# Five start offsets for the block weights of a two-block transformer kernel

## The reference, cut to what matters

```python
h = h + 0.5 * swiglu(rms_norm(h, ffn1_norm[i]), ffn1_w_in[i], ffn1_w_out[i])

def swiglu(x, w_in, w_out):
    g, u = jnp.split(x @ w_in, 2, axis=-1)      # w_in is 1024 x 5632: the up projection
    return (jax.nn.silu(g) * u) @ w_out         # w_out is 2816 x 1024: the down projection
```

## Time and profile before

| What | us |
|---|---|
| median of the two timed runs | 2789.9 (2788.57 to 2791.23) |
| profiled execution, its own time | 2787.86 |
| span of the profiled execution | 2786.1 |
| TensorE busy in the span | 2759.5 (99%) |
| weight loads (PEld) busy | 2358.5 (85%) |
| VectorE, ScalarE, GpSimd busy | 1657.8, 1338.5, 1570.1 |

### The profile page before, as it was taken

One profiled execution on the slowest core, in us unless ns is written; L12 is line 12 of the kernel. 1 busy time (PEld: TensorE's weight loads), 2 busy tenths in 40 slices (PEclk: granted clock), 3 DMA queues, 4 the chain that ended last, 5 costly groups with the idle time before them and its releaser, 6 DMA issues.

```text
span 2786.1 us, 45558 instructions
## 1 busy us (share of the span) xinstructions
PE 2759.5 (99%) x16386; PEld 2358.5 (85%) x16386; DVE 1657.8 (60%) x2703; ACT 1338.5 (48%) x2076; POOL 1570.1 (56%) x872
## 2 busy tenths in 40 slices
PE   8999999999999999999999999999999999999999
PEld 6998877899889998888999886765688888799987
DVE  6776147677616774135777316589788464467730
ACT  5554266555425553244555333566444444455531
POOL 6775445677547774444777443158633373377743
PEclk9999999999999999999999999999999999999999
DMA  3334322233322333332233331112222342123332
GB/s 138 108 119 113 93 85 81 92 116 110 104 92 93 117 113 98 101 107 84 94 117 121 96 109 62 54 46 68 76 84 74 101 151 76 54 92 117 115 99 77
DMA packets 80686, 267.91 MB, mean 96 GB/s; under 512 B 11169, under 2 KB 13217, under 8 KB 80561
## 3 DMA queue, kind: packets, MB, share of 16 engines
q1 hardware_dynamic: 77904, 262.01, 28.5%
q10 hardware_dynamic: 2656, 4.26, 0.5%
HBM read 263.09 MB, written 2.10 MB: 95 GB/s over the span
## 4 chain that ended last, share of the span: by engine, by line
PE 89%; DVE 5%; POOL 3%; ACT 2%; issue 1%; DMA 0%; DVEq 0%; ACTq 0%; SPq 0%
PE bank L467 17%; PE bank L469 16%; PE bank L468 16%; PE bank L723 10%; PE bank L725 9%; PE bank L724 9%; POOL xsum L814 1%; PE bank L556 1%; PE bank L554 1%; PE bank L555 1%; DVE xsum_f L900 1%; PE bank L1650 1%; PE bank L2062 1%; POOL ring_lo L810 1%; PE bank L2930 1%
## 5 line engine op out<-in xcount | busy, mean ns | idle before, releaser
L455 POOL TENSOR_TENSOR ring_lo<-w_stage,ring_hi 128x1024 fp32r<-128x1024 f32 (+1 forms) x228 | 535.9, 2356 | 712.9 <-ACT ring_hi L431 712.8
L431 ACT ACTIVATE ring_hi<-w_stage 128x1024 fp32r<-128x1024 f32 (+1 forms) x324 | 328.6, 1021 | 360.5 <-PE bank L469 298.9
L810 POOL TENSOR_TENSOR ring_lo<-w_stage,ring_hi 128x1024 fp32r<-128x1024 f32 (+1 forms) x176 | 326.1, 1853 | 176.1 <-ACT ring_hi L919 175.9
L467 PE MATMUL bank<-xg_hi,ring_hi 128*128 128x512 f32 x976 | 395.5, 405 | 4.0 <-DVE h_raw L1078 2.8
L462 POOL TENSOR_TENSOR ring_lo<-w_stage,ring_hi 128x1024 fp32r<-128x1024 f32 (+1 forms) x96 | 234.7, 2450 | 259.6 <-ACT ring_hi L431 215.2
L468 PE MATMUL bank<-xg_lo,ring_hi 128*128 128x512 f32 x976 | 380.6, 390 | 0.0
L469 PE MATMUL bank<-xg_hi,ring_lo 128*128 128x512 f32 x976 | 380.5, 390 | 0.0
L467 PE MATMUL bank<-h_hi,ring_hi 128*128 128x512 f32 x880 | 342.3, 389 | 0.0
L468 PE MATMUL bank<-h_lo,ring_hi 128*128 128x512 f32 x880 | 342.3, 389 | 0.0
L469 PE MATMUL bank<-h_hi,ring_lo 128*128 128x512 f32 x880 | 342.3, 389 | 0.0
L723 PE MATMUL bank<-xsum,s_w 128*128 128x256 f32 x1056 | 296.9, 281 | 0.7 <-DVE bank L1055 0.6
(11 more groups left out here) (531 smaller groups left out, 6682.0 us busy)
## 6 DMA issues: line engine op xcount, KB each, us to landing
w_stage<-w_up SPq DMA_DIRECT2D x220, 512.0 KB, 4.2
w_stage<-w_down SPq DMA_DIRECT2D x80, 512.0 KB, 3.5
w_stage<-merge SPq DMA_DIRECT2D x36, 512.0 KB, 3.4
w_stage<-w_down SPq DMA_DIRECT2D x40, 384.0 KB, 3.1
w_stage<-hg_qfg SPq DMA_DIRECT2D x12, 512.0 KB, 3.4
w_stage<-rec_r SPq DMA_DIRECT2D x8, 512.0 KB, 3.4
w_stage<-rec_y SPq DMA_DIRECT2D x8, 512.0 KB, 3.4
w_stage<-rec_out SPq DMA_DIRECT2D x8, 512.0 KB, 3.4
```

The costliest lines, as they stand in the source:

```text
L431: act.activation(w_hi[:, r, 0:w], w_stage[:, r, 0:w], ACT.Copy).then_inc(w_hi_ready, 1)
L455: pool.tensor_tensor(w_lo[:, r, 0:w], w_stage[:, r, 0:w], f32(w_hi[:, r, 0:w]), ALU.subtract).then_inc(w_lo_ready, 1)
L467: pe.matmul(out, w_hi[:, r, c], hi, start=start, stop=False)
L810: pool.tensor_tensor(wb_lo[:, r, cs], w_stage[:, r, cs], f32(wb_hi[:, r, cs]), ALU.subtract).then_inc(w_lo_ready, 1)
```

## The change

Each of the five up projections gets its own distance from the line: 8, 24, 32, 40 and 56 elements, which are 32, 96, 128, 160 and 224 bytes, for the first to the fifth. The distance applies to the block rows in both ring tiles and to S1, S3 and S2 alike, so that S2 moves from 192 bytes to the same distance as the others. All other tiles, the plain products, the instructions, their order and their semaphores stay as they are.

```diff
-    ASIDE = 16
+    BLOCK_ASIDE = (8, 24, 32, 40, 56)
...
-    wb_hi, wb_lo = slots(ring_hi, ASIDE), slots(ring_lo, ASIDE)
+    wb_of = [(slots(ring_hi, a), slots(ring_lo, a)) for a in BLOCK_ASIDE]
...
-    s3_w = place("s3_w", [P, 2, T], F32R, at=cursor[0] - 2 * T * 4 + 4 * ASIDE)
+    s3_of = [place(f"s3_w{i}", [P, 2, T], F32R, at=cursor[0] - 2 * T * 4 + 4 * a) for i, a in enumerate(BLOCK_ASIDE)]
...
-    s1_w = place("s1_w", [P, 2, T], F32R, at=work + 32 * KB + 4 * ASIDE)
-    s2_w = place("s2_w", [P, 2, T], F32R, at=work + 36 * KB + 12 * ASIDE)
+    s12_of = [(place(f"s1_w{i}", [P, 2, T], F32R, at=work + 32 * KB + 4 * a),
+               place(f"s2_w{i}", [P, 2, T], F32R, at=work + 36 * KB + 4 * a)) for i, a in enumerate(BLOCK_ASIDE)]
...
     def pe_ffn(pe, i, q):
+        (s1_w, s2_w), s3_w, (wb_hi, wb_lo) = s12_of[i], s3_of[i], wb_of[i]
...
     def pool_up(pool, U, i):
+        (s1_w, s2_w), s3_w, (wb_hi, wb_lo) = s12_of[i], s3_of[i], wb_of[i]
...
     def act_ffn(act, i, gain):
+        (s1_w, s2_w), s3_w, (wb_hi, wb_lo) = s12_of[i], s3_of[i], wb_of[i]
...
     def dve_ffn(dve, i, gain=None):
+        (s1_w, s2_w), s3_w, (wb_hi, wb_lo) = s12_of[i], s3_of[i], wb_of[i]
```

## The result

The changed kernel takes 2816.82 us (median of two runs, 2816.63 to 2817.0) against 2789.9: 26.9 us more, a ratio of 1.0091 with a 95% interval of 1.007 to 1.0111. The forecast was 2792 with a range of 2782 to 2812; the time lies above the range, close to rival C (2820).

What follows compares the result with a forecast made beforehand. TensorE's matmul pace bounds the kernel. Nothing for the pace, 2 us for cut rows and nothing for slower runs: 2787.9 + 2 = 2789.9 us as profiled, 2792 on the median's scale; range 2782 to 2812.

Steps and rivals of the forecast that it cites:

- rival C: Block stages: only whole multiples of 64 bytes are good, four stages go to 120 ns, 29.6 us more, 2820; chance 0.11.
- The bound and the reading of pace: Whole kernel: time is the number of matmuls times TensorE's pace; no other engine sets the pace in the block stages.
- I take 113.3 for all five: Block stages' matmuls: pace stays 113.3 ns at all five new distances, so nothing added; 32 bytes the weak point.
- rival B: Block stages: one or two distances fail (first or third stage), 7.1 or 7.5 us each, 2797 to 2807; chance 0.26.
- It looks like the price of the moving stream: All matmuls: the one in sixteen above the columns comes from the moving stream, which keeps its place.
- a hitch in the load is hidden beside 512 columns: Plain 512-column products: weight loads have time to spare, so a hitch shows only with 256 columns.
- rival D: Block stages: a distance better than 64 avoids the extra 6.7 ns, up to 49 us less, 2741; chance 0.10.
- The slower stretches of products: Block products paced at 117.8 ns behind waits, 90 of 616: 4 us less if gone, 4 more if doubled; taken as nothing.
- The rows cut by a 64-byte boundary: Weight loads at odd multiples of 32 bytes, four stages: nine pieces instead of eight, up to 4.9 us, 2 us taken.
- The loads' median as a sign: Weight loads of the block products: a median of 188 or 192 ns was to show whether a distance is good.
- ScalarE, VectorE, GpSimd at nothing: Engines touching the shifted tiles: distance costs them nothing; 18 us if VectorE's low parts got 10% longer without cover.
- A: Block stages: the forecast as summed, all stages together 4 us less to 9 us more, 2786 to 2799, at 2792; chance 0.53.

Runs made afterwards that it cites:

- e8: Kernel before with block rows alone moved to 16, 48, 80, 112 and 72 bytes, first to fifth stage: 2808.89 us.
- e10: Kernel before with block rows, S1, S3 at 64, 192, 320, 448, 64 bytes and S2 at 192, 320, 448, 576, 320: 2796.29 us beside 2793.22.
- e2: Kernel before with the plain products' weights moved from 0 to 64 bytes behind a line: 2828.04 us beside 2790.22.
- e5: Kernel before with the five down projections' weights at 32, 96, 128, 192, 160 bytes and xk's at 192: 2808.8 us against 2791.19.
- e1: Kernel before with one distance for all block weights in four stages (first 64, third 192, fourth 0, fifth 320 bytes), second stage unchanged: 2817.75 us.
- e9: Changed kernel with S2 moved to stand 128 bytes behind its neighbours in every stage: 2815.97 us.
- e3: Kernel before with the moving sums of x at 64, 64, 96, 32, 0 bytes by stage, and weights moved in the second and third stages: 2804.57 us.
- e4: Kernel before with block rows at 448, 128, 256, 64, 160 bytes, S1 and S3 at 448, 64, 256, 160, 64, S2 at 448, 192, 256, 160, 192: 2812.0 us.
- e7: Kernel before with all weights, the plain products' and S2's too, 64 bytes behind a line: 2843.92 us.

## Why the prediction was wrong

**The bound and the reading of pace: right.** TensorE's pace is all there is in these stages, and the whole 27 us came out of it: 88 steps at the new paces take 38.3 us more than 88 x 9.52 = 837.8, and 11.3 of these were waits and slower stretches before, as the forecast had split them. The price of a bad distance was right too: 120.0 ns gave 181.4 us in the fourth stage, as 18 x 10.08 had said.

**"I take 113.3 for all five": the step that failed.** The term for TensorE's pace was set at nothing; the five stages ran at 118.3, 117.5, 118.8, 120.0 and 117.9 ns. The term rested on two readings. The first was that 64 and 192 bytes, both good, bound a good stretch, with 96, 128 and 160 in it, so that only 32 was weak. e8 shows that 64 is a point: 48, 72 and 80 are at 118.0 to 118.8 ns. By e10 the pattern repeats, and two good values on a periodic quantity say nothing of what lies between them. The forecast saw in rival B that the good distances could repeat every 128 bytes, and yet priced that for the third stage alone.

**"It looks like the price of the moving stream": wrong, by e2 and e5.** The one column time in sixteen above the columns, at 512 as at 256 columns, grows with a bad distance: 226.7 to 233.3 ns. It is at least partly a matter of where the operands stand. The forecast's other reading, that a hitch in the load is hidden beside 512 columns, fell with it: those products lost 6.6 ns a matmul at 64 bytes (e2), about what xk gained. What is left above the columns at the best distance (6.7 and 13.3 ns) no placement here went below, so rival D found no support; whether some placement could isn't settled.

**The slower stretches of products: right that they are a matter of distance and phase, wrong that they were worth 4 us at most.** In the kernel before they were few, since each one ended at x22, behind S2 at 192. With that step gone a stage at 64 is slow from end to end: 158.3 in place of 154.1 us (e1, first stage). The change took this step away as well, which I had noted only as S2 moving; but by e9 this isn't what cost the time here.

**The rows cut by a 64-byte boundary (2 us): not borne out.** 128 bytes, which cuts nothing, is at 118.7 ns, worse than 32, 96 and 224, which do. **The loads' median as a sign (188 or 192 ns): no sign of the pace**, 188 ns at 120.0 in the fourth stage.

**ScalarE, VectorE, GpSimd at nothing: right**, 1053 and 692 ns for the first two, and GpSimd busy for 1569.9 us in place of 1570.1.

**The rivals.** C came nearest in its size, 2820 against 2816.8, and that is luck: its rule (whole multiples of 64 are good) fails in the third stage, where 128 bytes cost 5.9 us, and its four bad stages cost 21.0 us in place of 29.6, since only 160 bytes came to 120 ns. Two errors nearly cancelled. The chances leaned too far to the good side: with three known values of an unexplained quantity, of which one was bad, A and B, in which at least three of the five new ones are good, had 0.79 between them.

The Trainium skill's rule of two independent read ports ("SBUF — State Buffer", section "Who interferes with whom") would have the pace the same at every distance. The runs differ from it: twelve matmuls of one shape take 1.36 or 1.44 us by the distance between their two operands (e3, e4). Here the measurement decides. Which part of the memory or of TensorE the two streams meet in, no run shows.

## What to carry to other kernels

In this kernel, where each matmul has its own weight load and only 256 moving columns, the byte distance between the weights and the moving operand moves TensorE's pace by up to 6% (113.3 to 120.0 ns). Read it from the starts of matmuls in a stretch without waits, try single distances in one run with one value a stage, and don't infer one value from its neighbours. Try each width of moving operand by itself: 64 bytes is best for 256 columns and 3% slow for 512. And a good distance alone isn't enough: with all weights of a stage at 64 the pace was 117.8 ns (e1, first stage), no better than at 96; it took a product 128 bytes off in each step, placed so that the next one steps back from 192 to 64, to hold 113.3 ns for most of the time.

## What the hardware showed that I had not expected

- Two paces at the same addresses. At a distance of 64 bytes a stretch runs at 113.3 or at 117.8 ns a matmul and keeps to it, over 16 steps and 1344 matmuls in e1; a wait that puts two starts 0.19 us apart can push it from the fast to the slow one (e7, second stage), and once in these runs such a wait ended the slow one (e10, fifth stage).
- A step in distance from 192 to 64 bytes between two products ends the slow pace (117 of 120 passages), the step the other way never does (0 of 99), and a step of 256 bytes does nothing (0 of 26).
- The distance between operands counts, not the place of either: weights at 160 bytes run at 120.0 ns beside a moving operand at 0 and at 113.3 beside one at 96.
- With 512 columns the best of the distances tried is 0 (226.7 ns), then 192 (228.9), and the others lie at 232.4 to 234.3.
